# Latent attention with outputs of two heads on two 64-column tiles, from undivided probabilities

## The reference

```python
def mla_attend(qn, qr, kn, kr, v):
    scale = (MLA_NOPE + MLA_ROPE) ** -0.5
    s = jnp.einsum('bhqd,bhkd->bhqk', qn, kn) + jnp.einsum('bhqr,bkr->bhqk', qr, kr)
    p = jax.nn.softmax(s.astype(jnp.float32) * scale, axis=-1)
    return jnp.einsum('bhqk,bhkv->bhqv', p.astype(v.dtype), v)
...
        om_x = sweep_query_blocks(lambda a, b: mla_attend(a, b, kn, kr, vm), (qnx, qrx))
        ym_x = merge_heads(om_x)
        yf_x = fourier_mix(px[6])
        x = x + mx[5] * merge_branches(px[7], yd_x, ym_x, yf_x, w_branch_diff[l], w_branch_mla[l],
                                       w_branch_fourier[l], w_out[l])
```

## Time and profile before

| | us |
|---|---|
| median of 3 runs | 2196.85 |
| lowest and highest | 2193.18, 2198.25 |
| the profiled execution, its own time | 2197.59 |
| its span in the trace | 2195.6 |
| mean granted clock of PE | 0.992 |
| PE busy in the span | 2132.7 (97%) |
| DVE, ACT, POOL busy | 1395.0, 870.4, 68.0 |
| latent attention, layer 0 | from about 587 to 657 |
| latent attention, layer 1 | from about 1793 to 1899 |

### The profile page before, as it was taken

One profiled execution on the slowest core, in us unless ns is written; L12 is line 12 of the kernel. 1 busy time (PEld: TensorE's weight loads), 2 busy tenths in 40 slices (PEclk: granted clock), 3 DMA queues, 4 the chain that ended last, 5 costly groups with the idle time before them and its releaser, 6 DMA issues.

```text
span 2195.6 us, 30273 instructions
## 1 busy us (share of the span) xinstructions
PE 2132.7 (97%) x12076; PEld 1857.2 (85%) x12076; DVE 1395.0 (64%) x2388; ACT 870.4 (40%) x1495; POOL 68.0 (3%) x78
## 2 busy tenths in 40 slices
PE   6999999999999999999999999999999999999998
PEld 3888888987888888888888898888888888899998
DVE  5789986675573334566877556676647655467554
ACT  4321223545463223532222352222236545546444
POOL 0000001000000000100000000000010000000001
PEclk9999999999999999999999999999999999999999
DMA  7545554411112222334444324465533223254553
GB/s 277 202 167 179 209 185 129 147 63 46 49 64 97 101 88 80 116 135 144 165 180 156 123 97 143 131 205 201 178 101 118 78 87 111 97 194 172 177 199 124
DMA packets 75723, 302.49 MB, mean 138 GB/s; under 512 B 7488, under 2 KB 14400, under 8 KB 59200
## 3 DMA queue, kind: packets, MB, share of 16 engines
q1 hardware_dynamic: 56576, 233.21, 30.9%
q10 hardware_dynamic: 19008, 67.35, 8.8%
HBM read 296.35 MB, written 4.19 MB: 137 GB/s over the span
## 4 chain that ended last, share of the span: by engine, by line
PE 67%; DVE 4%; ACT 3%; issue 1%; DMA 1%; DVEq 0%; ACTq 0%
PE ps L612 20%; PE ps L614 20%; PE ps L613 20%; DVE w_lo L1853 1%; PE ps L1074 1%; ACT w_hi L1222 1%; PE ps L942 1%; PE ps L1128 1%; PE ps L928 0%; PE ps L1118 0%; DMA w_raw<-in_gate 0%; PE ps L950 0%; PE ps L931 0%; PE ps L930 0%; PE ps L672 0%
## 5 line engine op out<-in xcount | busy, mean ns | idle before, releaser
L1222 ACT CAST w_hi<-w_raw 128x1024 fp32r<-128x1024 f32 (+5 forms) x508 | 442.1, 879 | 983.0 <-PE ps L614 641.2
L612 PE MATMUL ps<-xn_hi,w_hi 128*128 128x512 f32 (+1 forms) x2272 | 803.0, 353 | 21.2 <-DVE xn_lo L2009 7.6
L1853 DVE TENSOR_TENSOR w_lo<-w_raw,w_hi 128x1024 fp32r<-128x1024 f32 (+5 forms) x508 | 512.9, 1014 | 475.7 <-ACT w_hi L1222 473.2
L614 PE MATMUL ps<-xn_lo,w_hi 128*128 128x512 f32 (+1 forms) x2272 | 792.7, 349 | 0.0
L613 PE MATMUL ps<-xn_hi,w_lo 128*128 128x512 f32 (+1 forms) x2272 | 792.6, 349 | 0.0
L612 PEld LDWEIGHTS ps<-xn_hi,w_hi 128*128 128x128 f32 x2272 | 432.7, 190 | 81.1 <-issue 18.0
L614 PEld LDWEIGHTS ps<-xn_lo,w_hi 128*128 128x128 f32 x2272 | 432.3, 190 | 55.1
L613 PEld LDWEIGHTS ps<-xn_hi,w_lo 128*128 128x128 f32 x2272 | 432.9, 191 | 52.6
L612 PE MATMUL ps<-split_scratch,w_hi 128*128 128x512 f32 (+2 forms) x1084 | 375.1, 346 | 2.6 <-DVE split_scratch L2071 1.0
L614 PE MATMUL ps<-split_scratch,w_hi 128*128 128x512 f32 (+2 forms) x1084 | 372.2, 343 | 0.0
L613 PE MATMUL ps<-split_scratch,w_lo 128*128 128x512 f32 (+2 forms) x1084 | 372.1, 343 | 0.0
(11 more groups left out here) (192 smaller groups left out, 1595.5 us busy)
## 6 DMA issues: line engine op xcount, KB each, us to landing
w_raw<-in_up SPq DMA_DIRECT2D x86, 1024.0 KB, 4.8
ada_w<-in_ada ACTq DMA_DIRECT2D x128, 512.0 KB, 4.6
w_raw<-in_dn SPq DMA_DIRECT2D x32, 768.0 KB, 4.8
w_raw<-in_merge SPq DMA_DIRECT2D x32, 768.0 KB, 4.4
w_raw<-in_dn SPq DMA_DIRECT2D x32, 640.0 KB, 4.3
w_raw<-in_proj SPq DMA_DIRECT2D x20, 1024.0 KB, 4.8
w_raw<-in_wout SPq DMA_DIRECT2D x16, 512.0 KB, 3.7
w_raw<-in_gate SPq DMA_DIRECT2D x8, 1024.0 KB, 5.0
```

Of the source, the lines that this page charges most:

```text
L612: nc.tensor.matmul(out, w_hi, hi, start=first, stop=False)
L614: return nc.tensor.matmul(out, w_hi, lo, start=False, stop=last)
L1222: nc.scalar.copy(wh[:, u % 2, h, 0:w], raw[:, u % RAW, h, raw_first(u + i * per):raw_first(u + i * per) + w]).then_inc(hi_ready, halves_of ...
L1853: nc.vector.tensor_tensor(wl[:, u % 2, h, 0:w], raw[:, u % RAW, h, raw_first(u + i * per):raw_first(u + i * per) + w], wh[:, u % 2, h, 0:w ...
```

## The change

Outputs are no longer made for each item but for a pair of heads and a stream (`head_pairs`, `pair_outputs`), eight groups in layer 0 and four in layer 1, three steps after the last item of the group. The values of a head (64 columns) are now the weights, on columns 0 to 63 of the array for the even head and 64 to 127 for the odd one, and the transposed probabilities of 256 queries stream through. The result has features on partitions, two heads on 128. It is not yet divided. For the division PE makes four small matmuls per group: the column of reciprocals, repeated 64 times, as weights, and the identity streaming, which lays the reciprocals of 128 queries along the free dimension on the 64 partitions of the head. ACT copies these 256 columns to `inverse_rows` (semaphore `rows_turned`), and DVE multiplies the outputs by them when it empties the bank, into `Y`. The transposes back, `YT` and `turned_back` go; the casts to `YMh` read `Y`, chunk by chunk on `o_ready`. The probabilities stay in larger homes (`turned_probs`) until the pair is done; in layer 0 part of these lies over `Of`, so ACT's first copies wait for `ydlo_ready` of POOL. The Fourier mix waits for `o_ready` ahead of its first inverse transform, no longer ahead of its first forward one.

```diff
-                def token_outputs(t):
-                    h, _, _, _, nk = items[t]
+                def pair_outputs(g):
+                    p, _, nk, t = groups[g]
+                    per = len(items) // MLA_HEADS
                     pe.wait_ge(wt_ready, a0 + t + 1)
                     banks = B_OT[l]
-                    if t >= len(banks):
-                        pe.wait_ge(o_ready, done["pair"] + t + 1 - len(banks))
+                    if g >= len(banks):
+                        pe.wait_ge(o_ready, done["pair"] + g + 1 - len(banks))
                     for kc in range(nk // P):
-                        ins = nc.tensor.matmul(ps[:, banks[t % len(banks)], 0:MLA_VD], WT4[:, t % 4, kc, :],
-                                               Vt[:, kc, h * MLA_VD:(h + 1) * MLA_VD],
-                                               start=(kc == 0), stop=(kc == nk // P - 1))
+                        for j in range(2):
+                            h, rows = 2 * p + j, slice(MLA_VD * j, MLA_VD * j + MLA_VD)
+                            out = ps[rows, banks[g % len(banks)], 0:2 * P].rearrange("p (t n) -> p t n", t=2)
+                            ins = nc.tensor.matmul(out, Vt[:, kc, h * MLA_VD:(h + 1) * MLA_VD], turned_probs(l, h, nk)[:, :, kc, :],
+                                                   start=(kc == 0), stop=(kc == nk // P - 1), tile_position=(0, MLA_VD * j))
+                    pe.wait_ge(inverse_ready, n0 + t + 1)
+                    for tq in range(2):
+                        for j in range(2):
+                            item = a0 + t - 1 + tq - per * (1 - j)
+                            ins = nc.tensor.matmul(ps[MLA_VD * j:MLA_VD * j + MLA_VD, banks[g % len(banks)], (2 + tq) * P:(3 + tq) * P],
+                                                   rr[:, item % 16, 0:1].to_broadcast([P, MLA_VD]), ident[:], start=True, stop=True,
+                                                   tile_position=(0, MLA_VD * j))
                     ins.then_inc(pv_done, 1)
...
-                    if t >= 3:
-                        token_outputs(t - 3)
+                    if pair_ended_by(l, t - 3) is not None:
+                        pair_outputs(pair_ended_by(l, t - 3))
...
-                cols = width(l < DEPTH - 1)
-                for c in range(4):
-                    pe.wait_ge(o_ready, done["pair"] - (3 - c) * 2 * len(item_list(l, 1)[0]))
-                    for tk in range(cols.start, cols.stop, P):
-                        ins = nc.tensor.transpose(ps[:, B_Y[c], tk:tk + P], YT[:, tk // P, c * P:(c + 1) * P], ident[:])
-                    ins.then_inc(turned_back, 1)
...
+                    g = pair_ended_by(l, t - 4)
+                    if g is not None:
+                        act.wait_ge(pv_done, done["pair"] + g + 1)
+                        if g:
+                            act.wait_ge(o_ready, done["pair"] + g)
+                        nc.scalar.copy(inverse_rows, ps[:, B_OT[l][g % len(B_OT[l])], 2 * P:4 * P]).then_inc(rows_turned, 1)
...
-                    act.wait_ge(turned_back, 4 * l + c + 1)
-                    nc.scalar.copy(YMh[:, c, cols], ps[:, B_Y[c], cols]).then_inc(ymhi_ready, 1)
+                    act.wait_ge(o_ready, done["pair"] - (3 - c) * len(streams(both)))
+                    nc.scalar.copy(YMh[:, c, cols], Y[:, c, cols]).then_inc(ymhi_ready, 1)
...
+                    g = pair_ended_by(l, t - 5)
+                    if g is not None:
+                        p, cols, _, _ = groups[g]
+                        dve.wait_ge(rows_turned, pairs_before(l) + g + 1)
+                        nc.vector.tensor_tensor(Y[:, p, cols], ps[:, B_OT[l][g % len(B_OT[l])], 0:2 * P], inverse_rows, ALU.mult
+                                                ).then_inc(o_ready, 1)
```

More of the change, by code:

```diff
@@ L457, in item_list, with head_pairs, pair_ended_by, probs_before @@
             return items, pairs
+        def head_pairs(l):
+            groups, per = [], len(item_list(l, 1)[0])
+            for p in range(MLA_HEADS // 2):
+                for c, (cols, nk) in enumerate([(LAT, TOK)] + ([(CTX, CTX_LEN)] if l < DEPTH - 1 else [])):
+                    groups.append((p, cols, nk, (2 * p + 1) * per + 2 * c + 1))
+            return groups
+        def pair_ended_by(l, t):
+            for g, (_, _, _, item) in enumerate(head_pairs(l)):
+                if item == t:
+                    return g
+            return None
+        def probs_before(l):
+            return sum(len(item_list(k, MLA_HEADS)[0]) for k in range(l))
+        def pairs_before(l):
+            return sum(len(head_pairs(k)) for k in range(l))
+        def turned_probs(l, h, nk):
+            if l == DEPTH - 1:
+                home = (SC[:, 0:1024], SC[:, 1024:2048], SD[:, 0:1024])[h % 3]
+            elif nk == TOK:
+                home = SC[:, 1024 * (h % 2):1024 * (h % 2) + 1024]
+            else:
+                home = SD[:, 512 * (h % 2):512 * (h % 2) + 512]
+            return home.rearrange("p (t k n) -> p t k n", t=2, k=nk // P)
+        def home_used(l, h, nk):
+            if l == DEPTH - 1:
+                return (h - 3) // 2 + 1 if h >= 3 else 0
+            return 2 * (h // 2 - 1) + (nk != TOK) + 1 if h >= 2 else 0
         def head_at(l, t):
@@ L1046, in mla_attention @@
             def mla_attention(l):
-                items, pairs = item_list(l, MLA_HEADS)
-                a0, g0 = done["item"], done["pair"]
+                items, groups = item_list(l, MLA_HEADS)[0], head_pairs(l)
+                a0, n0 = done["item"], probs_before(l)
                 mla_head(l, 1)
@@ L1095, in mla_attention @@
                 done["item"] += len(items)
-                done["pair"] += len(items)
+                done["pair"] += len(groups)
                 done["head"] += MLA_HEADS
-                cols = width(l < DEPTH - 1)
-                for c in range(4):
-                    pe.wait_ge(o_ready, done["pair"] - (3 - c) * 2 * len(item_list(l, 1)[0]))
-                    for tk in range(cols.start, cols.stop, P):
-                        ins = nc.tensor.transpose(ps[:, B_Y[c], tk:tk + P], YT[:, tk // P, c * P:(c + 1) * P], ident[:])
-                    ins.then_inc(turned_back, 1)
             def fourier(l):
                 both = l < DEPTH - 1
-                pe.wait_ge(o_ready, done["pair"])
                 pe.wait_ge(tables_loaded, 32 * (l + 1))
@@ L1122, in fourier @@
                         pe.wait_ge(ab_ready, k0 + t)
+                        if t == 1:
+                            pe.wait_ge(o_ready, done["pair"])
                         if k0 + t - 1 >= 2:
@@ L1644, in mla_attention @@
             def mla_attention(l):
-                items, pairs = item_list(l, MLA_HEADS)
-                a0, g0 = done["item"], done["pair"]
-                for t in range(-1, len(items) + 2):
+                items = item_list(l, MLA_HEADS)[0]
+                a0 = done["item"]
+                for t in range(-1, len(items) + 4):
                     if 0 <= t < len(items):
@@ L1670, in mla_attention @@
                 done["item"] += len(items)
-                done["pair"] += len(items)
+                done["pair"] += len(head_pairs(l))
             for v_ in range(2):
@@ L2447, in mla_attention @@
             def mla_attention(l):
-                items, pairs = item_list(l, MLA_HEADS)
-                a0, g0 = done["item"], done["pair"]
-                inverted = []
-                for t in range(-1, len(items) + 4):
+                items, groups = item_list(l, MLA_HEADS)[0], head_pairs(l)
+                a0 = done["item"]
+                for t in range(-1, len(items) + 5):
                     if 0 <= t < len(items):
```

38 lines of the change are left out of this document (16 added, 22 removed).

## The result

The changed kernel takes 2205.47 us (2202.43 to 2206.73) against 2196.85 (2193.18 to 2198.25): 1.0037 times the kernel before, interval 1.0025 to 1.0049. It is slower, by 8.6 us; I had said 2199, with 2189 to 2206 as the range. The profiled execution of the changed kernel has a span of 2203.7 us, that of before 2195.6, so the two traces differ by 8.1 us. In the changed kernel the lines are: 652 to 654 products, 982 transposes, 1102 to 1104 scores, 1118 outputs, 1124 reciprocals spread, 1161 and 1173 forward and inverse transforms; on ACT 1546 exp, 1698 copy of the gate bank, 1704 copy of the spread reciprocals, 1712 copy of turned probabilities, 1768 casts to YMh.

A forecast was written before the change was run, and what follows sets the result against it. PE, busy for 97% of the span, was taken as the bound, in layer 0's burst by only 0.36 us over ACT's copies. Layer 0 +3.9 and layer 1 -1.6 gave +2.3: 2199 us against 2196.85, range 2189 to 2206.

The forecast's parts named there:

- B: Layer 1, step 8: a PE wait of 2.05 us lowers PE's clock, +2.2 to 3 us, 2202; chance 22%.
- C: Pair outputs on PE: two column tiles overlap worse than four did, +4.5 us, 2204; chance 10%.
- Part 1: PE work in both layers: latent group 2.4 us, context group 1.5, balance about -9.8 us.
- D: Pair outputs on PE: column tiles don't overlap at all, +20 us, 2220; chance 5%.
- rival A: Both layers: only PE's work counts and ACT's chain of copies hides, -9.8 us, 2188; chance 20%.
- Part 2: Layer 0's bursts of steps: outputs, once spread evenly, now stand in lumped groups; sum +1.7 us.
- First burst: Layer 0's first burst of steps: outputs simply go, -0.7 us.
- bursts behind the 15-lump: Layer 0's bursts after a lump of 15 feature-product matmuls: each grows by 0.5 us with the context group.
- Behind the 9-lump: Layer 0's bursts after a lump of 9 feature-product matmuls: each grows by 0.7 us with the latent group.
- the last burst: Layer 0 from step 22: an existing PE wait of 1.10 us takes the latent group, cost 0.
- Part 3: End of layer 0: last latent group and casts behind the reciprocals' copy delay the first inverse transform, +2.2 us.
- Part 4: Layer 1: output bank wait goes, gate bank copy is next late, fewer outputs from step 13; -1.6 us.

The follow-up runs named there:

- l0_only: Changed kernel with the pair form in layer 0 alone and the token form in layer 1: 2205.69 us, 1.0041 times the kernel before.
- warm_l1: Changed kernel plus unread matmuls in layer 1, four at step 8 and seven at step 12: 2204.27 us, 1.0037 times the kernel before.
- after_again: The changed kernel itself, unaltered, measured once more: 2204.41 us, 1.0043 times the kernel before.
- after: The changed kernel in its first measurement and profile: 2205.47 us, 1.0037 times the kernel before.
- tail: Changed kernel with casts 0 to 2 ahead of the last pair's reciprocals copy, chunk 3's behind the first Fourier copy, both layers: 2205.71 us, 1.0044.
- l1_only: Changed kernel with the pair form in layer 1 alone and the token form in layer 0: 2197.06 us, 1.0001 times the kernel before.
- combo: Changed kernel with outputs spread over steps, ACT's order altered at the end, and unread matmuls in layers 0 and 1: 2198.64 us, 1.0008.
- warm_before: Kernel before plus five unread matmuls at step 12 of layer 1: 2193.45 us, 0.9984 times the kernel before.
- before_two_fills: Kernel before plus five unread matmuls at step 12 of layer 1 and five ahead of its step 0: 2194.88 us, 0.9989.
- warm_l0: Changed kernel plus unread matmuls in layer 0 at steps 3, 4, 29, 30 and 31, measured twice: 2205.94 us (1.0038) and 2206.38 (1.0040).

## Why the prediction was right or wrong, step by step

My likeliest case was "within 0.2%", 2199; the time came out slower by 0.4%, 0.5 us inside the upper end of the range. That it is inside is partly luck: the range reached so high for the sake of B and C; C didn't happen and B's price didn't come. The forecast was 6.5 us short of 2205.5, the difference 6.3 short (2.3 forecast, 8.6 measured).

**Part 1, PE work: right.** Predicted 2.4 and 1.5 us for the groups, measured 2.32 and 1.45. Sixteen passes of 256 columns on two column tiles take 1.78 us where 8 x 0.216 is 1.73: full overlap, so C and D are out. The Trainium skill's figure of 2.38 times for three column tiles (TensorE: Matmul & The Clock Gate, Part 3) would have meant about 2.2 us for these passes, by the estimate in my prediction; the measurement decides for full overlap of two. Entry costs 0.34 - 0.22 = 0.12 and exit 0.54 - 0.43 = 0.11 us, for my 0.25 in all. By start times the balance is 15.1 - 18.7 - 1.8 in layer 0 and 9.3 - 13.0 - 0.9 in layer 1, -10.0 for my -9.8. The page's busy time fell by 5.4 only: where PE stops, a row counts its whole duration, not the shorter distance to the next start, so more waits mean more busy time for the same work. The count of work was no guide to the time, and rival A (2188) is refuted: PE is busy 32.79 of 36.00 us.

**Part 2, the bursts: mechanism right, sizes short by 1.1 us.** First burst -0.70 for -0.7, bursts behind the 15-lump +0.51 and +0.48 for +0.5. Behind the 9-lump I had +0.7 and it is +0.94 and +0.93, and the last burst costs 0.64 where I had 0. Behind the 9-lump, the step that failed is that I let only copies hold PE: transposes 4 and 6 stand 3.04 us apart, for 3.27 before and 2.8 in my chain, because the scores between them wait 0.48 for the exp that frees their bank (0.66 in the burst shown). In the changed kernel such waits are 5.4 us, ten of them, before 2.4, two of them. I had named that as what would make me wrong. In the last burst the wait of 1.10 did take the latent group, as I said (the transposes of item 24 are 0.2 later), but I left out the context group behind them, which moves the next ones to 1.4 later, and only 0.75 of that comes back.

**Part 3, the end of layer 0: right at full clock, +2.16 for +2.2.** Its structure (last latent group ahead of the last transposes, casts behind the copy of reciprocals) is what the rows show. In the first profile it cost 4.85, since two pieces of low clock fell on it.

**What was missing in layer 0: the clock.** I looked for falls behind long waits in layer 1 and had none in my sum or rivals for layer 0. Here waits of 0.22 and 0.69 us between short rows (PE busy 1.09 of 2.00 us) stood ahead of the fall, and 0.55, 0.77 and 0.77 at the end. My row of 1.10 us with full clock behind it was no bound: the same code had full clock in one profile (l0_only), one piece in two (warm_l1 and after_again) and three in after. Segments of the same layer-0 code were 70.29, 71.96, 72.00 and 74.62, so the fall is worth 0 to 4.3 us, 1.9 on average over these four. A fifth profile of the same code, tail up to the transposes of item 31, has three pieces in the same places as after. The Trainium skill describes such a case (TensorE: Matmul & The Clock Gate, A second HAM failure mode: psum-queue depth-cycling): PE pausing briefly and often between groups of matmuls lets the clock swing. The rows agree; I had not weighed it.

**Part 4, layer 1: wrong, by about 2 us.** I had -1.6; layer 1 alone costs 0.2 +- 1.9 by the clocked runs, an interval that just takes in -1.6, so the times alone don't refute it; the rows do. The segment grew by 0.6 in after and by 1.9 in l1_only, and with three pieces of low clock, as many as before had in 103.71 us, it took 104.32 (after) and 103.27 (warm_l1). That the wait for the output bank goes and gate_taken is next late was right. But at step 12 I reckoned a gain of 0.9, and there is a wait of 3.64 us instead of 2.52. DVE's and ACT's timelines there, after:

```profile
1878.27 3.50 DVE L1906 TENSOR_TENSOR w_lo<-w_raw,w_hi 128x1024 fp32r<-128x1024 f32 x3 [0.21 <-ACT w_hi L1267]
1881.68 0.69 DVE L2369 TENSOR_REDUCE score_negmax<-ps 128x1 f32<-128x512 f32 x1
...
1882.41 0.69 ACT L1546 ACTIVATE x_res<-ps,score_negmax 128x512 f32<-128x512 f32 x1 [2.27 <-DVE score_negmax L2369]
```

Three splits, the maximum, the exp, the copy of the gate bank at 1883.09, and only then PE's gate products. This chain has the length that it had before, 5.88 us from ACT's first cast to the copy of the gate bank, and PE reaches its wait 0.4 us earlier in it. But the whole chain stands later: that copy starts 76.57 us after the segment's start, for 73.43 before. How the 3.1 us gather is only partly clear; in warm_l1, without the fall behind step 8 but with one behind step 4, they are 2.5. The outputs that are gone and one piece of low clock less behind step 12 win 2 us back: the transposes of item 15, which I put 1.3 us earlier, stand 98.48 us after the segment's start for 97.35 before, 1.1 later. From there to the inverse transform it is 5.84 for 6.36, a gain of 0.5 that I had at 0.3.

**Rival B: the event came, its price did not.** A wait of 2.17 us (2.05 forecast) at step 8 and low clock behind it. But keeping the clock up at steps 8 and 12 gave back 1.05 us in the segment against after, 2.1 for two pieces against after_again, and 1.2 (within the scatter) in the time. And before itself had paid for two pieces at step 12.

**The sum.** Sizes in layer 0 +1.1, layer 1 +1.8 (0.2 for -1.6), together 2.9 of the 6.3. The rest is about the 3.8 us between layer 0's 5.0 at full clock and the 8.8 by which layer 0's change alone is slower. The mean granted clock of every execution bears on what this is. Of 63 executions of the kernel before, 31 had 0.993, with a median of 2196.88 us; the one of l0_only with 0.993 took 2202.04 and the one of the changed kernel 2202.43, 5.2 and 5.6 us more, near the 5.0. The other four of l0_only and seven of the ten of the changed kernel had 0.990, which is 2 x 0.003 x 2204 = 13 us more low clock, about four pieces (my estimate), and l0_only's four took 3.6 to 4.4 us longer. So the missing term is, as far as these single executions show, low clock. Where it stands is not shown: the segment has 1.9 us of it on the four profiles, the first profile of the changed kernel has hardly more of it in all than that of before (39 us and 38, over the whole span), and the fills in layer 0, which took it out of the segment, did not lower the time.

What makes the pair form slow is plain all the same. Without the spreading of reciprocals it is 1.0005 of before; with it 1.0037 and 1.0043. The outputs in pairs save nothing that the times show: where PE's work shrinks, the chain of ACT and DVE holds the stage, as the two waits in the burst and the chain of step 12 show. The reciprocals add PE rows and an ACT copy in the steps where that chain ends last. Their price depends on where they stand, though: combo keeps all of them, spreads the outputs, alters ACT's order and fills the waits, and is 1.5 us over before. So 6.9 us is what they cost in this order, not a cost that any order would have.

## What to carry to other kernels

Work taken off PE inside a ring of copies, exps and waits comes back as waiting, and PE that waits in short pieces may be given half the clock: sum the ring (copy, exp, maximum, copy), not PE's rows, and charge for low clock as soon as PE stops being full (here 1 to 1.4 us for each piece). When a division is moved to the output side, price how the divisors get there: here it was 6.9 us of a loss of 7.4, where before the divisor had been a scalar operand of an evacuation that was needed anyway. The version that beats both kernels is the kernel before with five matmuls that nobody reads in its 2.52 us wait, 0.9984 (0.9975 to 0.9993); with a second such place it is 0.9989, so try each place singly. One profile of each kernel is not enough to say where low clock has gone: profiles of equal code differ by two or three pieces.

## What the runs showed of the chip that I had not expected

Two column tiles of 64 columns in fp32 run fully side by side: 1.78 us for 16 passes of 256 columns, 0.91 for eight. The stretches of low clock ahead of the last 12 us of the kernel amounted to 3.3 to 3.4, 6.8 or 10.2 us, and 3.4 of them were worth 1.39 us in layer 1's token form. Equal code and equal waits were followed by full clock in one execution and by half clock in another (2.35 us in step 4, 1.37 at the last output, 2.08 between the layers with no piece, one or three). Five matmuls of 256 columns in a wait kept the clock up behind it in every profile that has them (warm_before, before_two_fills; four and seven in warm_l1 and combo). Low clock then stood elsewhere in the profiles of warm_l1, both of warm_l0 and before_two_fills, but at 1826 (warm_l1) and from 922 on (warm_l0) it stands in profiles without fills too, so that the fills moved it is not shown.
